# A hybrid encoder layer: six PSUM banks for the first projection chunk, two weight pieces split before the last squares, and the first score product among the transposes

## The reference

```python
def rmsnorm(x, g=None):
    xf = x.astype(jnp.float32)
    y = xf * lax.rsqrt(jnp.mean(xf * xf, axis=-1, keepdims=True) + EPS)
    ...
def token_mixer(xn, w_in, ...):
    z = jnp.einsum('bsd,de->bse', xn, w_in)          # 1024 -> 5120 columns
    qa, ka, va, qr, kr, vr, gr, ga, gb = jnp.split(z, ...)
    oa = diff_attention(qa, ka, va, lam, subln_g, lam_init)
    ob = retention(qr, kr, vr, ret_decay_f, ret_decay_b)
    ob = jax.nn.silu(gr) * ob
    merged = jax.nn.sigmoid(ga) * (oa @ w_pa) + jax.nn.sigmoid(gb) * (ob @ w_pb)
    return merged @ w_out
# in diff_attention, per head and block of 128 queries, two score maps c = 0, 1:
    s = jnp.einsum('bhcqd,bhckd->bhcqk', qblk, k) * scale
    p = jax.nn.softmax(s, axis=-1)
    a = p[:, :, 0] - lam * p[:, :, 1]
    return jnp.einsum('bhqk,bhkv->bhqv', a, v)
```

## Time and profile before

| | |
|---|---|
| median of 3 runs | 1207.0 us (1206.47 to 1207.01) |
| the profiled execution: its time, its span | 1205.33 us, 1203.5 us |
| PE busy | 1093.9 us, 91% of the span |
| DVE busy, ACT busy | 520.1 us (43%), 400.6 us (33%) |
| mean granted PE clock | 0.967 of full speed |

### The profile page before, as it was taken

How to read it: one execution, slowest core, us unless ns; L and a number is a source line. 1 busy time by engine, 2 the same in 40 slices (tenths; PEclk the granted TensorE clock), 3 DMA queues, 4 the chain that set the end, 5 groups by cost and what they waited for, 6 DMA issues and landing times.

```text
span 1203.5 us, 15505 instructions
## 1 busy us (share of the span) xinstructions
PE 1093.9 (91%) x5142; PEld 660.6 (55%) x5142; DVE 520.1 (43%) x893; ACT 400.6 (33%) x629; POOL 189.1 (16%) x236
## 2 busy tenths in 40 slices
PE   5899999999999998999977999999998798999960
PEld 4688888888876667878863333333333233333320
DVE  5651522111027898563354435352443343341518
ACT  5322233222135666112214243424143323333232
POOL 0110011011000000000001232333233323232210
PEclk9999999999999999999987999999999999999995
DMA  8733331621341005448358899999999999999546
GB/s 312 256 123 123 114 122 48 240 104 44 139 170 58 1 2 175 158 152 360 123 219 357 351 422 419 419 420 420 420 413 420 421 421 419 419 422 419 225 158 260
DMA packets 69248, 308.89 MB, mean 257 GB/s; under 512 B 9024, under 2 KB 9152, under 8 KB 43872
## 3 DMA queue, kind: packets, MB, share of 16 engines
q1 hardware_dynamic: 56144, 273.86, 57.2%
q0 software_dynamic: 13072, 34.63, 7.4%
HBM read 278.57 MB, written 39.06 MB: 264 GB/s over the span
## 4 chain that ended last, share of the span: by engine, by line
PE 69%; DMA 14%; DVE 9%; ACT 4%; issue 3%; SPq 1%; DVEq 0%; ACTq 0%; POOLq 0%; POOL 0%
PE ps L869 18%; PE ps L584 12%; PE ps L586 12%; PE ps L585 12%; DMA rawe<-in_w 10%; PE ps L896 8%; DMA x_scratch<-x 2%; PE ps L859 2%; DVE cur13b L1662 1%; PE ps L878 1%; ACT prob L1013 1%; DMA xrow<-in_x_sample 1%; DVE att L1366 1%; ACT cur L1194 1%; DMA ya<-y_scratch 1%
## 5 line engine op out<-in xcount | busy, mean ns | idle before, releaser
L584 PE MATMUL ps<-whi,xTh 128*128 128x512 f32 x480 | 188.4, 393 | 18.1 <-DVE wlo L1225 13.8
L585 PE MATMUL ps<-wlo,xTh 128*128 128x512 f32 x480 | 187.9, 392 | 0.0
L586 PE MATMUL ps<-whi,xTl 128*128 128x512 f32 x480 | 187.9, 391 | 0.0
L869 PE MATMUL ps<-cur13a,xT 128*64 128x512 f32 x656 | 157.5, 624 | 2.0 <-DVE xT L1639 1.7
L1662 DVE COPY cur13a<-rawe 128x4096 f32 x31 | 71.2, 2296 | 191.3 <-DMA rawe<-in_w 99.7
L869 PE MATMUL ps<-cur13b,xT 128*64 128x512 f32 x656 | 147.8, 592 | 0.0
L896 PE MATMUL ps<-cur,hT 128*64 128x512 f32 x640 | 146.2, 598 | 0.0
L1194 ACT ACTIVATE cur<-rawe 128x4096 f32 x31 | 112.1, 3618 | 3.7 <-issue 1.4
L584 PEld LDWEIGHTS ps<-whi,xTh 128*128 128x128 f32 x480 | 91.0, 190 | 37.3 <-issue 18.5
L963 ACT ACTIVATE zst<-ps,rstd 128x512 f32<-128x512 f32 x60 | 41.1, 687 | 208.0 <-PE ps L586 205.9
L585 PEld LDWEIGHTS ps<-wlo,xTh 128*128 128x128 f32 x480 | 91.0, 189 | 19.1
(11 more groups left out here) (212 smaller groups left out, 1382.6 us busy)
## 6 DMA issues: line engine op xcount, KB each, us to landing
rawe<-in_w SPq DMA_DIRECT2D x96, 2048.0 KB, 25.9
raw<-in_w_in SPq DMA_DIRECT2D x20, 1024.0 KB, 6.2
z_scratch<-zst POOLq DMA_DIRECT2D x60, 256.0 KB, 2.3
gat<-z_scratch SPq DMA_DIRECT2D x12, 512.0 KB, 3.8
xn_scratch<-rrow POOLq DMA_DIRECT2D x6, 1024.0 KB, 5.2
ya<-y_scratch SPq DMA_DIRECT2D x6, 1024.0 KB, 10.7
raw<-in_w_out SPq DMA_DIRECT2D x4, 1024.0 KB, 6.6
xcol<-in_x_cols SPq DMA_DIRECT2D x6, 512.0 KB, 10.2
```

Of the source, the lines that this page charges most:

```text
L584: pe.matmul(out, ah, bh, start=first, stop=False)
L585: pe.matmul(out, ah, bl, start=False, stop=False)
L586: return pe.matmul(out, al, bh, start=False, stop=last)
L869: mm = pe.matmul(ps[0][u * CAP:(u + 1) * CAP, :], xT[:, c, h * CAP:(h + 1) * CAP], cur13[h][:, :, c * 512 + u * 256:c * 512 + u * 256 + 25 ...
```

## The change

It has three parts.

1. In chunk 0 the six row tiles go to the banks 0 to 5 (`ps[t]`), and PE waits for no copy there. In all other chunks banks and waits stay.
2. The pieces 2 and 3 (chunk 1) are split ahead of `square_row(4)` and `square_row(5)` on ACT, and on DVE right behind the last `input_lo`, ahead of the reciprocal root. Their places between the copies of chunk 0 go.
3. `scores(0)` is issued between the transposes of group 9 and 10, `maxes(0)` on DVE after its copy of group 9, `exps(0)` on ACT after its copy of group 10. The functions move ahead of their use in the text. The wait for all projection copies moves along with `scores(0)`, and two waits for the first four copies on each engine are added.

```diff
-                    bank = ps[(6 * m + t) % 4]
+                    bank = ps[t if isinstance(i, int) and m == 0 else (6 * m + t) % 4]
                     n = 12 * i + 6 * m + t
-                    if not (isinstance(i, int) and i == 0 and 6 * m + t < 4):
+                    if not (isinstance(i, int) and m == 0):
                         pe.wait_ge(s_zev, n - 3)
...
                 to_columns(f, ps[4 + f % 4])
-            pe.wait_ge(s_zev, NCH * NT)
+                if f == 9:
+                    pe.wait_ge(s_zev, NCH * NT)
+                    pe.wait_ge(s_qTa, 4)
+                    pe.wait_ge(s_qTd, 4)
+                    scores(0)
             pe.wait_ge(s_qTa, 9)
             pe.wait_ge(s_qTd, 9)
-            scores(0)
...
             input_hi(5)
+            hi_piece(2, 1, 2)
+            hi_piece(3, 1, 3)
             square_row(4)
             square_row(5)
...
                 c = 2 * i + m
+                bank = ps[t if c == 0 else k]
...
-                            if m == 0:
-                                hi_piece(2 + j, i + 1, 2 + j,
-                                         None if i == 0 else (s_zmm, 12 * i) if j else (s_pe, 2 * i))
-                            elif i + 1 < NCH // 2:
+                            if m == 0 and i > 0:
+                                hi_piece(2 + j, i + 1, 2 + j, (s_zmm, 12 * i) if j else (s_pe, 2 * i))
+                            elif m == 1 and i + 1 < NCH // 2:
...
+            act.wait_ge(s_zmm, NCH * NT)
+            for f in range(0, 18, 2):
+                act.wait_ge(s_qT, f + 1)
+                act.activation(qk_columns(f), ps[4 + f % 4][:, :], ACT.Copy).then_inc(s_qTa, 1)
+                if f == 10:
+                    exps(0)
...
-            exps(0)
             for n in range(NIT):
...
+            lo_piece(2, 2, 3)
+            lo_piece(3, 3, 4)
             dve.wait_ge(s_par, 16 * 7)
...
-                            if m == 0:
+                            if m == 0 and i > 0:
                                 z_lo(i, 2 + t // 2)
...
+            for f in range(1, 18, 2):
+                dve.wait_ge(s_qT, f + 1)
+                dve.tensor_copy(qk_columns(f), ps[4 + f % 4][:, :]).then_inc(s_qTd, 1)
+                if f == 9:
+                    maxes(0)
...
-            maxes(0)
             for n in range(NIT):
```

More of the change, by code:

```diff
@@ L961, in z_out @@
                         act.wait_ge(s_zro, ROTS + t - 1)
-                    act.activation(sgz[t % 2][:, :], ps[k][:, :], ACT.Sigmoid, scale=rstd[:, t:t + 1])
-                act.activation(zst[k][:, :], ps[k][:, :], ACT.Sigmoid if c >= 6 else ACT.Copy,
+                    act.activation(sgz[t % 2][:, :], bank[:, :], ACT.Sigmoid, scale=rstd[:, t:t + 1])
+                act.activation(zst[k][:, :], bank[:, :], ACT.Sigmoid if c >= 6 else ACT.Copy,
                                scale=rstd[:, t:t + 1]).then_inc(s_zev, 1)
@@ L991, in qk_columns @@
                 return v.rearrange("p h n -> p (h n)")
[L992 to L999, removed]
-                q = n_sq[0]
-                n_sq[0] += 1
-                if q >= 4:
-                    act.wait_ge(s_osq, q - 3)
-                act.activation(sqj[:, q % 4, :], src, ACT.Square, accum_out=ssq[:, col:col + 1]).then_inc(s_osq, 1)
             def exps(n):
@@ L1016, in exps, with square @@
                 e.then_inc(s_ex, 1)
+            act.wait_ge(s_zmm, NCH * NT)
[4 more added lines that the diff above has]
+                    exps(0)
+            n_sq = [0]
+            def square(src, col):
+                q = n_sq[0]
+                n_sq[0] += 1
+                if q >= 4:
+                    act.wait_ge(s_osq, q - 3)
+                act.activation(sqj[:, q % 4, :], src, ACT.Square, accum_out=ssq[:, col:col + 1]).then_inc(s_osq, 1)
             def squares(n):
@@ L1342, in qk_columns @@
                 return v.rearrange("p h n -> p (h n)")
[L1343 to L1346, removed]
             def maxes(n):
@@ L1354, in maxes @@
                 dve.tensor_scalar(nm[:, n % 2, :], mx[:, n % 2, :], -HD ** -0.5, None, ALU.mult).then_inc(s_mx, 1)
+            dve.wait_ge(s_zmm, NCH * NT)
+            for f in range(1, 18, 2):
[3 more added lines that the diff above has]
+                    maxes(0)
             def weights(n):
```

## The result

The changed kernel takes 1198.56 us (median of 4 runs, 1197.80 to 1198.97). The kernel before, run again beside it, takes 1207.01 us (1206.47 to 1207.92). The ratio is 0.9933 with an interval of [0.9919, 0.9946]: faster by 8.4 us, where 5.9 were forecast. The direction was right, the size was not.

A forecast was written before the change was run, and what follows sets the result against it. It took PE's projection pause for the first PSUM copy, and the DVE and ACT chain pacing attention, as the bounds the change touches. A + B = 5.99 - 0.1 = 5.9 us; 1207.0 - 5.9 = 1201.1 us, range 1199.3 to 1203.0.

The forecast's parts named there:

- Part A: First projection stage: six banks and early splits remove PE's 4.47 us pause and 1.52 us slow restart, 5.99 us.
- rival 3: First stage: the 4.47 us stall only moves, chunk 1 waiting for splits or copies; 1204.1 us with half gone; chance 0.04.
- rival 4: First stage: slower, late piece 3 holds ACT, squares, scale and banks once it lands after 37.0; chance 0.02.
- So the two edits that reorder splits and squares cost nothing, and they are needed: First stage: early splits delay the scale beside matmuls with 2 us to spare; otherwise piece 3's split comes too late.
- Part B's chain at the full clock: Transposes to attention loop: first score among the transposes lets second maxima start 0.91 us earlier at 2.4 GHz.
- The waits of 1.65 and about 0.9 us: Transposes: new PE pauses, about 1.65 us for ACT's copy of group 12 and 0.9 us before scores 1.
- The wait of 0.35 us for group 11's copy: Transposes: PE waits 0.35 us after group 14 because DVE copies group 11 only after the first maxima.
- The clock in part B: Scores 1: short new pauses drop PE to 1.2 GHz, as in an expert-loop row near 658; 1.0 us lost.
- B: Net gain of the first score moved among the transposes: 0.91 - 1.0 = -0.1 us.
- rival 1: Scores 1: the clock stays at 2.4 GHz, gain +0.91 us, total time 1200.1 us; chance 0.30.
- It hurt nothing there: Attention start: clock fall to 1.2 GHz behind the 2.8 us pause called harmless, scores 2 being ready in time.
- The median of the runs is 1.67 us above it: Whole kernel: median lies 1.67 us above the profiled 1205.33 us, so the forecast starts from 1207.0 us.

The follow-up runs named there:

- A alone: Kernel before with parts 1 and 2 of the change; the first score stays behind the transposes: 1201.30 us, ratio 0.9956.
- part 1 alone: Kernel before with six banks only; the splits of pieces 2 and 3 stay between the copies: 1201.32 us, ratio 0.9944.
- the filled pause: Five useless matmuls in PE's pause before the first attention weights: added to parts 1 and 2, 1199.09 us; added to the kernel before, 1206.99 us.
- the two fastest versions: Change with exponential table loaded after group 8, exponentials 0 after group 12, scores 1 ahead of the last waits: 1196.52 us; same without part 2: 1196.37 us.

## Why the prediction was off

- **Part A, 5.99 us: right, within what the profiles tell.** The projection stage became 5.69, 5.91 and 6.31 us shorter than the 334.34 of the first profile before, in three profiles of the change, and with A alone 5.65; against the 335.13 of the second profile each is 0.8 us more. In the medians A alone brings 5.4. Neither rival 3 nor rival 4 came: piece 3 was there for ACT at 35.82, before the 37.0 from which the slower case begins.
- **"So the two edits that reorder splits and squares cost nothing, and they are needed": half wrong.** They cost nothing beside six banks; they are not needed (part 1 alone, 1201.32 us against 1201.30). This did not change the sum.
- **Part B's chain at the full clock: right.** The waits of 1.65 and about 0.9 us came as 1.69 and 0.87, the gain of 0.91 as 0.97. The wait of 0.35 us for group 11's copy did not come: PE goes through groups 10 to 15 without a pause.
- **"The clock in part B" failed.** It took scores 1 at 1.2 GHz, from one row of the expert loop. The prediction read that row as a case of short repeated idles, but it is none: PE had worked from 649.65 to 657.4 us without a pause, and stood still once, for 1.57 us. The clock stayed at 1.00 in three profiles of three, so B was +0.97 and not -0.1: 1.07 us of the miss. This is rival 1.
- **"It hurt nothing there" failed.** That sentence, on the fall behind the pause of 2.8 us, was read off one execution, in which the fall lasted 3.4 us. In the other four profiles of kernels that leave this pause open it lasted 6.8 or 10.2 us, and attention took 113.4 to 114.7 us. Part B ends the long pause and with it this fall; the sum had no term for that. With parts 1 and 2 the filled pause alone gives 2.2 us.
- **"The median of the runs is 1.67 us above it" was carried to the change.** The profiled execution of before was 1.67 us faster than its median, that of the change 0.41 slower than its own. Between the two profiled executions the difference is 6.36 us, near the forecast's 5.9; the other 2.08 us of the 8.44 are these two offsets. In the second profile of the kernel before, with the longer fall, the time (1206.57) lies at its median (1206.52). So the offset was a sign that the profile read was not the usual execution.

In the medians the miss of 2.5 us divides so: parts 1 and 2 brought 5.4 us where 5.99 were forecast (0.6 less), and part 3 on top of them 3.0 where -0.1 was forecast (3.1 more). Of these 3.1, 1.07 are the clock at scores 1. The other 2.0 are what is left for the end of the fall behind the long pause, and the filled pause, which ends this fall without part 3, brings 2.2. That holds on six banks. It is not shown on four: there, neither part 3 nor the filled pause moved the median, though their profiles show attention at 110.28 and 111.70 us.

The runs of all four-bank kernels spread wide (1202.4 to 1210.6 us), those of the change from 1197.5 to 1200.4 (14 runs), of the two fastest versions from 1195.0 to 1196.8 (10 runs). Part of the wide spread goes with the granted clock. Of the 63 runs of the kernel before beside the experiments, the 21 with a mean clock of 0.964 or more have a median of 1205.5 us, the 30 with 0.962 or less one of 1207.8. In part 1 alone one of the six runs took 1197.04 us, at a mean clock of 0.967, the other five 1200.97 to 1202.42 at 0.961 to 0.964. In which stage a run lost its clock is not known, and the clock does not account for the filled pause on four banks, whose runs have a median clock of 0.9655 and still take 1206.99 us. What else varies on four banks is open. What decides how long the clock stays down, or whether it falls at all, was not settled.

## What to carry to other kernels

Behind a pause of PE, look at the granted clock and its length in more than one profile before a fall is put down as harmless: a loop that hides 3.4 us at the lower clock may not hide 6.8 or 10.2. Filling such a pause with work that nobody reads is a cheap test of what the fall costs; it showed 2.2 us in one kernel here and nothing in the other. The offset of one profiled execution from the median belongs to that execution, and is not carried to the changed kernel.

## What the runs showed of the hardware

- Behind the pause of 2.8 us the granted clock was at 1.2 GHz for 3.4, 6.8 or 10.2 us; two profiles of the same program (before) gave 3.4 and 6.8, both six-bank kernels with the pause open 10.2.
- Behind waits of 1.69 and 0.88 us with about 1 us of transposes between, the clock fell to 1.2 GHz in one of five profiled executions, for 6.8 us; in the others it stayed at 2.4.
- The load of ACT's table took 1.28 us, and a one-column exponential 0.20 us; moved to where ACT had time (the two fastest versions), neither stands in a wait of PE.
